# Three buffers of one weight stream, sized anew: 6/3/3 places become 4/4/4

## The reference

```python
h = rmsnorm(x, norm_g)
qa, ka, va, iq, ik, iw, qb, kb, vb, gate = split_cols(h @ w_in, SPLIT0)
...
return x + (y * jax.nn.silu(gate)) @ w_out
```

## Time and profile before

| | |
|---|---|
| median of 3 runs | 2296.97 us (2296.95 to 2297.91) |
| the profiled execution | 2295.67 us, its span 2293.9 us |
| busy share of the span | PE 95%, PEld 78%, DVE 68%, ACT 47%, POOL 5% |
| mean granted clock of TensorE | 0.989 of 2.4 GHz |
| HBM read and written | 421 MB and 57 MB, 209 GB/s over the span |
| the chain that ended last | PE 66%, DVE 19%, DMA 6%, ACT 4%, issue 4% |

### The profile page before, as it was taken

How to read it: one execution, slowest core, us unless ns; L and a number is a source line. 1 busy time by engine, 2 the same in 40 slices (tenths; PEclk the granted TensorE clock), 3 DMA queues, 4 the chain that set the end, 5 groups by cost and what they waited for, 6 DMA issues and landing times.

```text
span 2293.9 us, 35232 instructions
## 1 busy us (share of the span) xinstructions
PE 2188.8 (95%) x14268; PEld 1795.8 (78%) x14268; DVE 1550.6 (68%) x2298; ACT 1070.6 (47%) x1490; POOL 115.4 (5%) x188
## 2 busy tenths in 40 slices
PE   7999989999999999999999999998899999989997
PEld 6889668888788788887777777777687778767886
DVE  5665475657997455667999696665865566667754
ACT  5444466455444656554343463333554333345443
POOL 0000001001001001000000100001010000011000
PEclk9999999999999999999999999999999999999999
DMA  7666337857778556858665753338687334477763
GB/s 241 184 191 189 96 105 262 292 195 231 265 275 294 189 173 234 334 183 284 212 225 170 256 191 118 127 127 331 221 296 269 125 121 131 148 291 250 251 192 121
DMA packets 222481, 481.14 MB, mean 210 GB/s; under 512 B 14896, under 2 KB 51552, under 8 KB 217584
## 3 DMA queue, kind: packets, MB, share of 16 engines
q1 hardware_dynamic: 200112, 372.91, 49.0%
q0 software_dynamic: 22208, 105.99, 12.6%
HBM read 421.45 MB, written 57.40 MB: 209 GB/s over the span
## 4 chain that ended last, share of the span: by engine, by line
PE 66%; DVE 19%; DMA 6%; ACT 4%; issue 4%; POOL 0%; ACTq 0%; DVEq 0%; SPq 0%; POOLq 0%
PE mm_acc L308 37%; PE mm_acc L312 19%; DVE mm_lo L213 6%; DMA mm_raw<-in_w_in 1%; ACT mm_hi L206 1%; DVE mix_mub L1884 1%; DVE s_q L3003 1%; DVE s_p L2988 1%; DVE s_r L2996 1%; DVE s_p L2989 1%; DVE s_r L2998 1%; DMA rwk_src<-rw_rh 1%; PE in_turn L412 1%; PE rwk_bank L2438 1%; PE even_lg_ps L1027 1%
## 5 line engine op out<-in xcount | busy, mean ns | idle before, releaser
L213 DVE TENSOR_TENSOR mm_lo<-mm_raw,mm_hi 128x1024 fp32r<-128x1024 f32 (+4 forms) x672 | 789.9, 1184 | 478.0 <-ACT mm_hi L206 468.2
L206 ACT CAST mm_hi<-mm_raw 128x1024 fp32r<-128x1024 f32 (+4 forms) x672 | 680.7, 1019 | 731.6 <-PE mm_acc L312 694.1
L308 PE MATMUL mm_acc<-mm_hi,mm_aT_hi 128*128 128x512 f32 (+5 forms) x2208 | 862.2, 391 | 16.7 <-ACT mm_hi L206 16.6
L308 PE MATMUL mm_acc<-mm_hi,mm_aT_lo 128*128 128x512 f32 (+5 forms) x2208 | 852.8, 387 | 0.0
L312 PE MATMUL mm_acc<-mm_lo,mm_aT_hi 128*128 128x512 f32 (+5 forms) x2208 | 598.6, 388 | 14.9 <-DVE mm_lo L213 14.6
L308 PEld LDWEIGHTS mm_acc<-mm_hi,mm_aT_hi 128*128 128x128 f32 x2208 | 418.3, 189 | 97.1 <-ACT mm_hi L206 17.3
L312 PEld LDWEIGHTS mm_acc<-mm_lo,mm_aT_hi 128*128 128x128 f32 x2208 | 408.9, 189 | 94.5 <-DVE mm_lo L213 22.9
L308 PEld LDWEIGHTS mm_acc<-mm_hi,mm_aT_lo 128*128 128x128 f32 x2208 | 418.9, 190 | 72.0 <-issue 4.5
L308 PE MATMUL mm_acc<-mm_hi,in_yT_hi 128*128 128x512 f32 x256 | 100.9, 394 | 0.3 <-ACT mm_hi L206 0.3
L308 PE MATMUL mm_acc<-mm_hi,in_yT_lo 128*128 128x512 f32 x256 | 99.7, 389 | 0.0
L258 ACT ACTIVATE mm_stage<-mm_acc,mm_row_scale 128x512 f32<-128x512 f32 (+3 forms) x104 | 64.4, 672 | 75.1 <-PE mm_acc L312 75.1
(11 more groups left out here) (633 smaller groups left out, 2059.9 us busy)
## 6 DMA issues: line engine op xcount, KB each, us to landing
mm_raw<-in_w_in SPq DMA_DIRECT2D x384, 512.0 KB, 5.1
mm_raw<-in_w_out SPq DMA_DIRECT2D x96, 512.0 KB, 5.6
mm_raw<-in_w_in SPq DMA_DIRECT2D x72, 464.0 KB, 4.1
mm_raw<-in_w_branch SPq DMA_DIRECT2D x48, 512.0 KB, 5.6
proj<-mm_stage SPq DMA_DIRECT2D x46, 512.0 KB, 3.1
mm_raw<-in_w_in SPq DMA_DIRECT2D x32, 416.0 KB, 4.6
home_tab<-s5t_tab POOLq DMA_DIRECT2D x4, 2048.0 KB, 9.5
s_tab<-home_tab POOLq DMA_DIRECT2D x8, 1024.0 KB, 6.2
```

The lines of the kernel that those rows point to most:

```text
L206: self.nc.scalar.copy(self.hi[:, c % RING, :, 0:t.w], self.raw[:, c % RAW, :, 0:t.w]).then_inc(self.hi_done, 1)
L213: self.nc.vector.tensor_tensor(self.lo[:, c % RING, :, 0:t.w], self.raw[:, c % RAW, :, 0:t.w], self.hi[:, c % RING, :, 0:t.w].bitcast(F32) ...
L308: last = nc.tensor.matmul(self.acc[s][m][:, 0:t.w], t.aT[a][:, k0 + k, m * P:(m + 1) * P], self.hi[:, c % RING, k, 0:t.w], start=(k0 + k = ...
```

## The change

Three constants: the places for raw weights (`RAW`), those for high and for low parts (`RING`), and how many chunks beyond its count ACT casts and DVE subtracts (`AHEAD`). `AHEAD` also stands in `Pace.lead`, and `RAW` in the number of loads that SP offers beyond its count (`RAW - 1`) and in the seam's first loads (`prefetch`).

```diff
 TN, KC = 512, 2
 HIGH, STEPS = 4 * KC, 6 * KC
-RAW, RING, AHEAD = 6, 3, 2
+RAW, RING, AHEAD = 4, 4, 3
```

## The result

The changed kernel takes 2481.26 us (median of 4 runs, 2468.24 to 2493.20) beside 2297.44 us for the kernel before: the ratio is 1.0789 [1.0766, 1.0813], 184 us slower. The prediction was 2343, its range 2304 to 2398. The direction was right, the time is 83 us above the range.

A forecast was written before the change was run, and what follows sets the result against it. TensorE, busy 2188.8 of 2293.9 us, was taken as the bound. Start 4.0, contended ends 11.4 and a further 49, mostly stands in chains, less a gain of 18, made +46 on 2297.0: 2343 us, range 2304 to 2398.

The forecast's parts named there:

- the stand: At a plain tile end, ACT waits 4.9 us at the fourth chunk's cast for a load queued behind the store.
- the clock: Rival: half-clock stretches behind some eight new PE waits of 3 us and more, 1.5 us each: +12, 2355 us; chance 0.07.
- start: First seam: DVE weighs the second block 4.0 us later, at 19.4 us, behind chunk 3's subtraction; PE waits as long.
- contended ends: Ten tile ends where PE is full and other transfers delay the load: 11.4 us lost in all.
- seams: Turned blocks of the two seams, whose norm DVE brings later: 4 us lost.
- S5 scan: 1050 to 1290 us, DVE full: a lag of 3 us, paid once, then covered by the extra chunk.
- the gain of 18: One more chunk in hand at PE's waits for high and low parts, 14 us, plus 4 us from Pace.lead.
- The share I take by how much PE idles on such chains now: Stands in attention, convolution, inverses and RWKV chains: part of the full 127 us, scaled by PE's present idling.
- the queue at 1573 us: Tile end whose first load behind the store took 17.3 us: 3 us lost, not the rule's 11.
- The rival "in full": All stands in chains, 127 us, reach PE: +131 us, 2428 us; chance 0.13.
- Pace.lead: In the inverses and RWKV, it may run PE one chunk further while a chain is awaited: 4 us gained.
- The sign "some 60" waits of ACT: ACT's waits for raw weights rise from 16 to some 60, of 4 to 5 us each, just behind an evacuation.

The follow-up runs named there:

- e1: The changed kernel with six loads offered beyond SyncE's count instead of three, ahead of the store's wait: 2306.61 us, ratio 1.0041 to the kernel before.
- e4: The kernel before with RAW alone taken from 6 to 4, so three loads are offered instead of five: 2363.25 us, ratio 1.0283.
- e3: The kernel before, all its places kept, with three loads offered beyond SyncE's count instead of five: 2362.74 us, ratio 1.0273.
- e2: The changed kernel with four loads offered beyond SyncE's count instead of three: 2347.72 us, ratio 1.0218 to the kernel before.
- e7: The changed kernel with AHEAD back at 2 (RAW 4, RING 4, three loads offered): 2360.79 us, ratio 1.0270 to the kernel before.
- e10: The kernel before with four loads offered beyond SyncE's count instead of five: 2314.57 us, ratio 1.0070.
- e9: The kernel before with RAW taken from 6 to 4 and six loads offered instead of five: 2320.97 us, ratio 1.0088.
- e6: The kernel before with seven loads offered beyond SyncE's count instead of five: 2287.99 us, ratio 0.9958.

## Why the prediction was wrong

The mechanism held: the queue, the position at the fourth chunk, the length of the stand, and its cause (e1). What failed are sizes, by stretch, and a term left out of the sum, the clock. The losses by the prediction's terms, and measured at the same matmuls; e4 and e1 stand beside for what the offer alone does, and the change without the stand:

| stretch of before, us | predicted loss | after | e4 | e1 |
|---|---|---|---|---|
| start | 4.0 | 6.2 | 0.3 | 6.4 |
| 280 to 360, even attention | 8 | 11.8 | 0.0 | 0.0 |
| 360 to 980, contended ends 11.4, odd attention 7, seams 4 | 22.4 | 72.4 | 42.5 | 7.1 |
| 1050 to 1290, S5 scan | 3 | 0.8 | 0.0 | -2.9 |
| 1300 to 1400, convolution | 9 | 28.3 | 4.0 | 0.7 |
| 1400 to 1550, inverses | 4 | 6.7 | -1.7 | -3.0 |
| 1550 to 1640, preparation | 7 | 12.3 | 7.1 | 0.9 |
| 1640 to 2000, RWKV | 7 | 42.2 | 7.7 | 2.8 |
| sum | 64.4 | 180.7 | 59.9 | 12.0 |

The other stretches add 2 us after the change. 64.4 less the gain of 18 made the predicted +46. The span grew by 137 us more than that. Of these, 52 are busy time of PE; 64 are idle time in three stretches beyond what was forecast for them (360 to 980, convolution, RWKV); and 18 are the gain, which did not show.

1. **The step that failed: "The share I take by how much PE idles on such chains now".** It made 39 us of the 127 that the stands in chains would cost in full (the 49 hold 3 for the S5 scan, 4 for the seams and 3 for the queue at 1573 us besides). By idle time alone it came out in four stages: 8.9 us in the even attention (8 predicted), 8.5 in the odd one (7), 4.1 in the inverses (4), 7.4 in the preparation (7, with the 3 of the queue). It failed in the convolution, 24.8 us for 9, and in RWKV, 26.7 for 7, where the full price was 18.8 and 49 (10 x 4.9). The clock took another 3.5 and 15.5 us there. The idle share of PE in the kernel before says how much slack the chain leaves there; it says nothing of a stand that comes ahead of a step which PE awaits at a fixed place of its program. The RWKV end shows it: PE had 4 us of work behind the tile's end, then `rwk_beT`. Chunks in hand don't help, because PE's program does not pass over a chain step to the next chunk. The predicted RWKV loss is near what e4 loses (7.7): there the stand lies behind the step. Why the convolution lost more than its full price was not taken apart.

2. **The rival "in full" had the idle time, not the time.** It gave +131 us; PE's idle time rose by 130.7. That the two agree to a microsecond is chance. The chains paid 80 us of idle time by the stages above, not 127; late casts and seams outside them, and the gain that did not show, made up the rest.

3. **The clock was mis-sized, and stood outside the sum.** The prediction kept it as a rival, +12. It came out at +52.2 us of busy time for the same matmuls, 48 of it in matmuls that ran, in one kernel or the other, while the clock stood at its lower level; it is the largest single part of the 137 us. At the even attention's 5.92 us wait the granted clock fell to 0.50, the 1.2 GHz level, about 2 us before the wait ended, and stayed there for 10 us (PE's wait, and the stretch):

```profile
300.93 0.79 PE L487 MATMUL even_lg_ps<-even_qkT 128*128 128x128 f32 x2 [5.92 <-DVE even_lg L549]
...
299.00:309.00 10.00, 6.77 (x22) 5.71 (x23) 8.33 (x33) 5.71 (x15) 0.00 (x0) 0.50 0.54 168
```

   PE was busy for 6.77 us of them at half speed, so some 3.4 us were lost beside the wait (an estimate from this row); the prediction took 1.5 us from one short example. Over the span each added microsecond of idle time came with 0.40 of added busy time (52.2 / 130.7); in e3 it was 0.44 (20.2 / 45.6) and in e2 0.43 (16.3 / 38.3). It is no constant: the other runs with late loads lie between 0.29 (12.4 / 43.4, e7) and 0.51 (8.6 / 16.9, e10), those with the loads first are scattered more widely still. The Trainium skill (TensorE: Matmul & The Clock Gate, "Why this matters for your kernels") says to leave no long idle gaps between bursts of matmuls. The trace agrees, with the 0.50 of the row above. In a chained stage such a loss belongs into the sum.

4. **Contended ends and seams were too small.** In the stretch of 360 to 980 us PE idles 62.6 us where it idled 11.3. Its largest waits there after the change:

```profile
PE mm_acc L308 <- ACT mm_hi L206: 23.3, 11, 10.6
PE in_turn L412 <- DVE in_at L782: 9.0, 3, 5.1
PE odd_turn L1225 <- DVE odd_w L1333: 7.3, 2, 5.9
```

   For casts PE waits 23.3 us (1.7 before), where the contended ends had 11.4; for the turned blocks of the seams 11.0 (none before), where they had 4; for the odd attention's own steps 14.9 (6.4 before), 7 predicted. The tables of S5, for which the prediction had no term, make 5.4 (0.9 before). PE's busy time makes 21.2 of the 72.4 (608.70 to 629.93 us), with the granted clock down from 1.00 to 0.96. Later landings are not the cause in general: the median of 4.6 us did not change, and the load of 17.3 us at 1573 us took 4.5. One end alone makes 10.6 of the 23.3 us: in the odd attention the load issued at 786.25 took 12.6 us (at the same end of the kernel before, the first load behind the store took 8.1), and PE stood for 10.6 us. The cast and PE's wait, and the landings of that load and of the store ahead of it:

```profile
798.89 1.04 ACT L206 CAST mm_hi<-mm_raw 128x1024 fp32r<-128x1024 f32 x1 [13.08 <-DMA mm_raw<-in_w_in]
...
799.99 0.80 PE L308 MATMUL mm_acc<-mm_hi,mm_aT_hi 128*128 128x512 f32 x1 [10.62 <-ACT mm_hi L206]
...
mm_raw<-in_w_in SPq DMA_DIRECT2D x1, 512.0 KB, 12.6
proj<-mm_stage SPq DMA_DIRECT2D x1, 416.0 KB, 10.6
```

   With the loads first (e1), 7.1 of the 72.4 us are left.

5. **The gain: it did not show in the changed kernel, and *Pace.lead* gave nothing.** PE's waits for low parts fell from 14.6 to 8.4 us, as meant; those for casts rose from 16.9 to 37.5, for the raw weights were late. In e1, with the stand gone, PE waits 19.7 us for both where it was 31.5: 11.8 us gained, 14 predicted. The chunk in hand is worth what was said once the stand is gone. The 4 us of *Pace.lead* were nothing: PE's instructions stand in the same order in both kernels.

6. **The start** was right in place and nearly in size. The weighing came at 19.78 us, predicted 19.4, behind the subtraction of chunk 3 (DVE):

```profile
18.74 1.12 DVE L213 TENSOR_TENSOR mm_lo<-mm_raw,mm_hi 128x928 fp32r<-128x928 f32 x1 [2.92 <-ACT mm_hi L206]
19.78 1.22 DVE L792 TENSOR_TENSOR in_at<-in_xt,in_gw 128x1024 f32<-128x1024 f32 x1
```

   The tile ended 6.2 us later instead of 4.0; the matmuls behind it still took 0.59 us where they took 0.38 before, so part of the difference is their slower pace. The clock's records begin only behind them.

7. **The S5 scan** lost 0.8, predicted 3.

8. **The sign "some 60" waits of ACT** held for the fourth chunk alone (56). The other 172 of the 228 waits, 193 us, the prediction did not foresee. With the loads first, four raw places have 45 waits (e9) and six have 8 (e6), so the four places have a part in them.

## What to carry to other kernels

When a queue issues loads and stores in order, ask which load stands first behind a store's wait, and who asks for it how soon; offering loads further, ahead of that wait, was worth 175 us here, and 9 us in the kernel that had no such fault to show. A stand on an engine in front of TensorE is priced by what stands behind it in that engine's program and where TensorE awaits it, not by today's idle share: one place sooner turned 7.7 us of RWKV into 42. Count a wait of several microseconds in a chain once as a wait and, by the runs with late loads here, 0.3 to 0.5 of it again for the clock.

## What the runs showed of the hardware that was not expected

The first load behind a store landed as fast with three loads offered as with five: over the 56 stores the median was 4.6 us in both kernels, and single landings reached 17.3 us before and 12.6 after, among a stage's other transfers. Each of the ten waits of TensorE of 5 to 6 us in the changed kernel had the granted clock fall to 0.50, the 1.2 GHz level, before it ended; at the even attention's wait it stayed there for 10 us in all. In the kernel before the one wait of that length (5.6 us) did the same.
